# A two-tile feed-forward opened tile by tile with the tokens stationary, and the last norm's weight splits held back

## The reference

```python
def conv_glu_ffn(h, w_up_act, w_up_lin, w_conv, b_conv, w_down):   # first block, layers 0 and 1
    a = causal_depthwise_conv(h @ w_up_act, w_conv, b_conv)        # 3 taps over the tokens
    return (jax.nn.gelu(a) * (h @ w_up_lin)) @ w_down
...
def _swiglu(h, wg, wu, wd):                                        # second block
    return (jax.nn.silu(h @ wg) * (h @ wu)) @ wd
```

## Time and profile before

| | us |
|---|---|
| median of 3 runs | 2521.29 (2520.06 to 2528.47) |
| the profiled execution, its own time | 2527.51 |
| its span in the profile | 2525.7 |
| TensorE busy in it | 2431.3 |
| DVE busy in it | 1676.3 |
| ACT busy in it | 1080.5 |

### The profile page before, as it was taken

One profiled execution on the slowest core, in us unless ns is written; L12 is line 12 of the kernel. 1 busy time (PEld: TensorE's weight loads), 2 busy tenths in 40 slices (PEclk: granted clock), 3 DMA queues, 4 the chain that ended last, 5 costly groups with the idle time before them and its releaser, 6 DMA issues.

```text
span 2525.7 us, 34847 instructions
## 1 busy us (share of the span) xinstructions
PE 2431.3 (96%) x13166; PEld 2048.0 (81%) x13166; DVE 1676.3 (66%) x2618; ACT 1080.5 (43%) x1850; POOL 393.7 (16%) x431
## 2 busy tenths in 40 slices
PE   6899999999999999999979999999999999999998
PEld 5678987779989888887648888888888888787997
DVE  6957886857995776777865464566465566356454
ACT  4556545566554213237745322224322224345543
POOL 1111101111111201115851110110100110001101
PEclk9999999999999999999989999999999999999999
DMA  8755886646783654453212363442353444432662
GB/s 313 249 171 189 291 305 213 211 145 228 255 279 117 204 188 167 173 178 93 67 34 84 133 185 133 152 175 99 128 197 125 160 170 113 123 91 74 197 196 92
DMA packets 135880, 422.57 MB, mean 167 GB/s; under 512 B 28448, under 2 KB 32672, under 8 KB 135712
## 3 DMA queue, kind: packets, MB, share of 16 engines
q1 hardware_dynamic: 135152, 418.55, 49.0%
q10 hardware_dynamic: 560, 1.79, 0.2%
HBM read 419.17 MB, written 1.11 MB: 166 GB/s over the span
## 4 chain that ended last, share of the span: by engine, by line
PE 66%; DVE 2%; ACT 1%; POOL 1%; issue 0%; POOLq 0%; DVEq 0%; ACTq 0%
PE ps L1141 20%; PE ps L1142 20%; PE ps L1143 20%; PE ps L1336 2%; PE ps L1324 1%; POOL ap L2208 1%; PE ps L1241 1%; PE ps L1293 1%; PE ps L1304 1%; DVE ps L2033 0%; PE ps L1359 0%; PE ps L1348 0%; ACT F L1458 0%; DVE sl L1687 0%; DVE hL L1776 0%
## 5 line engine op out<-in xcount | busy, mean ns | idle before, releaser
L1399 ACT ACTIVATE sh<-raw 128x1024 fp32r<-128x1024 f32 x534 | 551.5, 1043 | 916.9 <-PE ps L1143 884.4
L1141 PE MATMUL ps<-hH,sh 128*128 128x256 f32 (+1 forms) x2560 | 843.1, 329 | 3.9 <-DVE hL L1776 2.9
L1143 PE MATMUL ps<-hH,sl 128*128 128x256 f32 (+1 forms) x2560 | 838.4, 327 | 0.0
L1142 PE MATMUL ps<-hL,sh 128*128 128x256 f32 (+1 forms) x2560 | 838.3, 327 | 0.0
L1687 DVE TENSOR_TENSOR sl<-raw,sh 128x1024 fp32r<-128x1024 f32 x534 | 639.4, 1217 | 100.6 <-ACT sh L1399 100.0
L1141 PEld LDWEIGHTS ps<-hH,sh 128*128 128x128 f32 x2560 | 481.4, 188 | 55.7 <-issue 8.1
L1143 PEld LDWEIGHTS ps<-hH,sl 128*128 128x128 f32 x2560 | 483.4, 189 | 48.1
L1142 PEld LDWEIGHTS ps<-hL,sh 128*128 128x128 f32 x2560 | 482.2, 188 | 49.1 <-issue 1.7
L1701 DVE CUSTOM_DVE_ANT_0 mjunk<-raw,cB,V 128x1024 bf16<-128x1024 f32 x384 | 499.0, 1299 | 27.0 <-DMA C<-in_cst 8.4
L2181 POOL TENSOR_TENSOR uLl<-F,uHh 128x256 fp32r<-128x256 f32 (+1 forms) x132 | 167.7, 1270 | 1185.0 <-ACT uHh L1576 1077.2
L1141 PE MATMUL ps<-sh,uHh 128*128 128x512 f32 x792 | 312.8, 395 | 2.1 <-DVE sl L1687 2.0
(11 more groups left out here) (164 smaller groups left out, 2047.3 us busy)
## 6 DMA issues: line engine op xcount, KB each, us to landing
raw<-in_w SPq DMA_DIRECT2D x752, 512.0 KB, 4.6
G<-gates SPq DMA_DIRECT2D x14, 512.0 KB, 6.3
raw<-in_w SPq DMA_DIRECT2D x16, 256.0 KB, 4.3
cB<-in_rpb SPq DMA_DIRECT2D x64, 64.0 KB, 2.6
raw<-in_w SPq DMA_DIRECT2D x4, 492.0 KB, 6.1
S<-in_rows SPq DMA_DIRECT2D x6, 256.0 KB, 3.3
X<-in_x ACTq DMA_DIRECT2D x1, 1024.0 KB, 11.9
X<-in_ctx SPq DMA_DIRECT2D x1, 1024.0 KB, 6.0
```

Source lines behind the costliest of these rows:

```text
L1141: self.e.matmul(out, lh, rh, start=start, stop=False)
L1142: self.e.matmul(out, lh, rl, start=False, stop=False)
L1143: return self.e.matmul(out, ll, rh, start=False, stop=stop)
L1399: self.e.activation(self.m["sh"][k % SPL][:, 0:w], self.m["raw"][r % RAW][:, 0:w], ACT.Copy).then_inc(self.sems["w_hi"], 1)
```

## The change

1. `by_tile` opens the two-tile feed-forwards in place of 14 fillers, `finish_norms()` and 5 fillers. It takes the first four 128-feature chunks of both weight matrices as 8 units of two row blocks x 512 columns, and multiplies with h stationary, tile by tile, as `down` does: units 0 to 3 (first matrix) and 4, 5 (second) for tile 0, then all for tile 1 in between with the rest of tile 0. Tile 1's turn and hsplit (`finish_norms`) stand behind the third part. Each [128 tokens, 512 features] result is copied from its bank to an S buffer (`utok`: tile 0 on ACT, tile 1 on DVE) and turned by four transposes into the banks that the products used to fill (`uturn`), two chunks to a bank.
2. In `ffn1` chunks 4 to 21 follow as products as before. The convolution and gelu of chunks 0 to 3 are put into chunks 4 and 5; the last transposes stand behind chunk 4's first product. In `ffn2` chunks 0 to 3 have their silu and multiplication ahead of chunk 4's products.
3. The fillers ahead are 7 in `ffn1` and 14 in `ffn2`.
4. At the end of the mixers of the first block, uppers are held from tile 1's first w_out part to `by_tile`. One is let through behind tile 0's hsplit, which now stands ahead of tile 1's `gate2`, and one ahead of tile 1's scale, where the first one's lower stands too.

```diff
@@ norm_tile
+        if held:
+            self.add("lowers")
+            self.add("ready", n=1)
         ys = [self.place("S", j) if wide else self.next("PT", 2) for j in range(2)]
         self.add("scale", t=t, st=st, ys=ys, xs=[self.xs(t, 0), self.xs(t, 1)])
@@ gate_half
         self.first_parts()
         self.rms_close(st2[t], 2)
+        self.second_parts()
+        if held and t:
+            self.add("ready", n=1)
@@ mixer
                     part(kp, half, taken[(kp, half)], [i], i == 1, banks[half][i] if kp == 3 else None)
-                self.gate_half(i, half, banks[half][i], gid, AB, hid, st2)
+                    if i and not half and kp == 2:
+                        self.add("hold", on=True)
+                self.gate_half(i, half, banks[half][i], gid, AB, hid, st2, True)
@@ new
+    def by_tile(self, names, hid, warm):
+        take = lambda n, j: self.unit(True, [n + (k, 0, 512) for k in (2 * j, 2 * j + 1)])
+        def part(n, j, t, b, last):
+            self.add("down", unit=n, ks=[2 * j, 2 * j + 1], tiles=[(t, (t, b))], last=last, full=b if j == 3 else None,
+                     act=("h", hid), nk=KD)
+            if t:
+                self.pace()
...
+        self.warm(warm)
+        self.add("hold", on=False)
+        one, two = ([take(n, j) for j in range(4)] for n in names)
+        A, B = [self.bank(), self.bank()], [self.bank(), self.bank()]
+        for j in range(3):
+            part(one[j], j, 0, A[0], False)
+        self.finish_norms()
+        part(one[3], 3, 0, A[0], False)
+        for j in range(2):
+            part(two[j], j, 0, B[0], False)
+        SA0 = stage(0, A[0], "a")
+        to = [self.bank(), self.bank()]
+        for j in range(4):
+            part(one[j], j, 1, A[1], True)
+            if j == 1:
+                turned(0, SA0, to)
+        for j in range(2):
+            part(two[j], j, 1, B[1], True)
+        SA1 = stage(1, A[1], "v")
+        for j in range(2, 4):
+            part(two[j], j, 0, B[0], False)
+        turned(1, SA1, to)
+        SB0 = stage(0, B[0], "a")
+        for j in range(2, 4):
+            part(two[j], j, 1, B[1], True)
+        up = [self.bank(), self.bank()]
+        turned(0, SB0, up)
+        SB1 = stage(1, B[1], "v")
+        return to, up, lambda: turned(1, SB1, up)
@@ ffn1
-        self.warm(14)
-        self.finish_norms()
-        self.warm(5)
+        to, up, rest = self.by_tile((("w_up_act", l), ("w_up_lin", l)), hid, 7)
         self.aside += [lambda: None] * 8
...
-        for c in range(KF):
+        for c in range(4, KF):
             ba = self.product("w_up_act", l, c * 128, slice(0, 256), ("h", hid))
-            if late:
+            if c == 4:
+                rest()
+            if c in (4, 5):
+                while late:
+                    late.pop(0)()
+                begin(2 * c - 8, to[c - 4], up[c - 4], 0)
+            late.pop(0)()
+            bu = self.product("w_up_lin", l, c * 128, slice(0, 256), ("h", hid))
+            late.pop(0)()
+            if c in (4, 5):
+                begin(2 * c - 7, to[c - 4], up[c - 4], 256)
                 late.pop(0)()
...
+            begin(c, ba, bu, 0)
             self.pace(2)
@@ ffn2
-            self.warm(14)
-            self.finish_norms()
-            self.warm(5)
+            to, up, rest = self.by_tile((("ffn_w_gate_2", (l, half_i)), ("ffn_w_up_2", (l, half_i))), hid, 14)
...
+                if len(tiles) == 2 and cc < 4:
+                    ba, bu, o = to[c // 2], up[c // 2], 256 * (c % 2)
+                    if c == 0:
+                        rest()
...
@@ finish
+                    if split and held and not (real and n <= s["unit"]):
+                        if not more:
+                            break
+                        more -= 1
@@ Tensor
+    def uturn(self, s):
...
+        self.wait_ge(self.got("tok", s["S"]))
+        for c in range(4):
+            o = 256 * (c % 2) + 128 * t
+            x = self.e.transpose(self.buf(s["to"][c // 2])[:, o:o + 128], S[:, c * 128:(c + 1) * 128],
+                                 self.m["C"][:, C_ID:C_ID + 128])
@@ Scalar
+    def utok(self, s):
...
+        self.e.copy(self.buf(s["S"])[:, :], self.buf(s["b"])[:, :]).then_inc(self.sems["a_ps"], 1)
@@ Vector
+    def utok(self, s):
...
+        self.e.tensor_copy(self.buf(s["S"])[:, :], self.buf(s["b"])[:, :]).then_inc(self.sems["v_ps"], 1)
```

More of the change, by code:

```diff
@@ L207, in xs, with norm_tile @@
         return ("x", t, h, self.x_at[(t, h)])
-    def norm_tile(self, hid, t, AB, s, st=None, wide=False, lag=0, early=False):
+    def norm_tile(self, hid, t, AB, s, st=None, wide=False, lag=0, early=False, held=False):
         if st is None:
@@ L310, in products, with gate_half @@
         return [b for _, b in got]
-    def gate_half(self, t, half, b, gid, AB, hid, st2):
+    def gate_half(self, t, half, b, gid, AB, hid, st2, held=False):
         if half == 0:
@@ L331, in gate_half @@
                 st = self.rms_open(self.xs(t, 0), D)
-        self.norm_tile(hid, t, AB, 0, st, early=True)
+        self.norm_tile(hid, t, AB, 0, st, early=True, held=held and t)
     def bias_rows(self, row, gid, tiles, hid):
@@ L627, in ffn2 @@
                 begun = bool(head)
+                if len(tiles) == 2 and cc < 4:
+                    ba, bu, o = to[c // 2], up[c // 2], 256 * (c % 2)
+                    if c == 0:
+                        rest()
+                    g = dict(N=N, c=c, ba=ba, bu=bu, o=o, s=self.place("S", c % 2), f=self.next("F", 3), fid=fid, u=self.u_at)
+                    if late:
+                        late.pop(0)()
+                    self.add("glu2_a", **g)
+                    if c % 2:
+                        self.left(ba, bu)
+                    late.append(lambda g=g: self.add("glu2_b", **g))
+                    continue
                 if head:
@@ L900, in finish @@
         out, n, ctx, top, used, order, lower, loads = [], 0, False, 0, set(), [], [], []
+        held, more = False, 0
         for s in self.steps:
             real = "unit" in s and s["kind"] != "place"
+            if s["kind"] == "hold":
+                held, more = s["on"], 0
+                continue
+            if s["kind"] == "ready":
+                more += s["n"]
+            if s["kind"] == "lowers":
+                out += lower
+                lower = []
+                continue
             if real:
@@ L905, in finish @@
                 lower = []
-            if "unit" in s or "upto" in s:
+            if "unit" in s or "upto" in s or s["kind"] == "ready":
+                if s["kind"] == "ready":
+                    s["upto"] = len(self.units)
                 top = max(top, s["upto"] if "upto" in s else s["unit"] + 1)
@@ L1169, in warm @@
         self.done("mm", ("left", s["b"]))
+    def uturn(self, s):
+        t, S = s["t"], self.buf(s["S"])
+        if t == 0:
+            for b in s["to"]:
+                self.wait_ge(self.gone(b))
+        self.wait_ge(self.got("tok", s["S"]))
[3 more added lines that the diff above has]
+                                 self.m["C"][:, C_ID:C_ID + 128])
+        x.then_inc(self.sems["tr"], 1)
+        self.done("tr", ("left", s["S"]), *([("full", b) for b in s["to"]] if t else []))
     def proj(self, s):
@@ L1978, in oscale @@
         self.done("v_sb", ("os", s["mid"], s["kd"], s["i"]))
+    def utok(self, s):
+        if s["on"] != "v":
+            return
+        self.wait_ge(self.got("full", s["b"]))
+        self.wait_ge(self.gone(s["S"]))
+        self.e.tensor_copy(self.buf(s["S"])[:, :], self.buf(s["b"])[:, :]).then_inc(self.sems["v_ps"], 1)
+        self.done("v_ps", ("left", s["b"]), ("tok", s["S"]))
     def glu1_a(self, s):
         l, c, fid = s["l"], s["c"], s["fid"]
-        S, pa = self.buf(s["s"]), self.buf(s["ba"])
+        S, pa = self.buf(s["s"]), self.buf(s["ba"])[:, s["o"]:s["o"] + 256]
         self.wait_ge(self.got("glu_a", fid, c))
```

47 lines of the change are left out of this document (30 added, 17 removed).

## The result

The changed kernel takes 2542.47 us (median of 6 runs, 2540.23 to 2543.43) against 2522.44 (median of 6, 2520.06 to 2528.47): a ratio of 1.0079, with an interval of 1.0065 to 1.0093. It is 20 us slower; the forecast was 2513.5, with 2506 to 2518.5 as its range and 0.05 for "slower".

The account below looks back on a forecast made before the run. TensorE, 96% busy, was taken to set the time behind layer 0's opening, DVE behind layer 1's. Gains 6.2 - 0.8 + 2.4 = 7.8 us, taken from the median 2521.3, gave 2513.5; range 2506 to 2518.5.

Parts of the forecast that it names:

- slower: Rival: the openings' matmuls run at the lower clock, 1.2 GHz, 22 us a place, up to 2579; chance 0.05.
- What A owes later: Layer 0's feed-forward: DVE's deferred convolution and gelu of chunks 0 to 3 are repaid at 0.87 us a chunk, costing nothing.
- A's margin: Layer 0's feed-forward: DVE ends unit 16's lower 1.5 us before TensorE wants it (8.6 before the change).
- the queue at B: DVE's work behind layer 1's opening: 8.0 us of idle counted, unit 16's lower at 620.1, TensorE stalling some 4.6 us.
- DVE without gaps of its own: Sign in layer 1's feed-forward: DVE runs gapless while TensorE idles 4 to 5 us for a lower.
- Place A: End of layer 0's mixer, before its two-tile feed-forward: gains 6.2 us, bounds 4.8 to 7.2.
- Place B: The same place in layer 1: loses 0.8 us as DVE decides; bounds +6.9 and -3.5.
- Place C: Before the last feed-forward, its norm unchanged: gains 2.4 us (1.4 to 2.9).
- A is eaten too: Rival: DVE's debt passes the 1.5 us margin in layer 0, TensorE stalls at unit 16, about 2518; chance 0.17.
- The Trainium skill's drain: Layer 1's silu table load: 1.38 us of drain per switch would lengthen the ping-pong by 1.4, losing 2.2 there.
- the gates' transfer: Layer 1: SP waits 8.8 us for the gates' columns ahead of weight loads, starving ACT 7.29; now four chunks later.

Follow-up runs that it names:

- e1: Changed kernel with the limit put back: the steps letting an upper through no longer raise the modulation columns' limit; 2513.47 us, ratio 0.997 to the kernel before.
- e6: Kernel before with the new opening and its norm in layer 1 alone, the limit put back; 2521.70 us, ratio 1.0002.
- e3: Kernel before with the opening by tile in the last feed-forward only; 2517.69 us, ratio 0.9989.
- e2: Kernel before plus the raised limit alone, so columns place the next upper from layer 0's first product on; 2538.01 us, ratio 1.0065.
- e4: Changed kernel with SP's fetch of the first block's feed-forward gates put three chunks behind its send; 2537.39 us, ratio 1.0063.

## Why the prediction was wrong

**The step that failed** is in "What A owes later": "DVE's saturated period is (624.02 - 620.51) = 3.5 us for a chunk without a modulation column, and 6.04 with one of two streams". These periods belong to an order of lowers, multiplication and convolution that the change does not keep. I took `ready` for "one upper let through", as the change says, and not also for a raised limit that stays. With the periods went "DVE wins back 5.65 - 3.5 - 1.28 = 0.87 us a chunk" (measured: it loses 0.1), and with them both A's margin and the queue at B. None of my rivals had it: the "slower" one was the clock in the openings, and it stayed at 1.00 there. Of the prediction's signs it is "DVE without gaps of its own" that the changed kernel fails, with 0.94 us in each chunk.

**What held, once the order was right (e1).** The total: 2513.5 forecast, 2513.47 measured. That is in part luck, since the terms differ as follows.

- *Place A* was to gain 6.2, with the opening's end 30.3 us behind tile 0's transposes. e1 has 31.1 (last transposes at 235.99, 0.35 for them, one product of 2.8 inside). Tile 1 is ready 15.6 us behind those transposes, not 14.9, and TensorE, through with tile 0's parts 0.7 later than forecast, waits 0.94 for it, as forecast. Against the profiled execution of before the gain is 5.4; at equal pitch it is 3.9 to 4.6, because the eight products replaced cost 21.8 rather than 22.6.
- *Place B*: a wait of 4.6 us for unit 16's lower, 26.9 us behind the opening's end, was forecast. e1 has 4.57, at 610.80, 26.7 behind 584.1. The forecast for the whole place was 0.8 lost; e1 and e6 have between 0.3 lost and 3.9 won, so better. A loss that I had not priced is the clock behind that wait: 0.66 in the 5 us from 610.
- *Place C*: 2.4 forecast, 2.4 in the changed kernel and in e3, at the slower pitch for the kernel before.
- *The rival "A is eaten too"* has the right place (unit 16's wait is at 255.23 in the changed kernel, with 0.63 us) and the wrong size: not a debt once, but a rate below TensorE's for the rest of the stage.
- *The Trainium skill's drain* beside ACT_TABLE_LOAD (ScalarE: Activation LUTs, What ACT_TABLE_LOAD costs) would, by an estimate, have put e1's wait at 6.0 instead of 4.57; the trace agrees with the row and not with that figure. In e1 too the silu's table load starts 0.02 us behind ACT's previous end, and the silu 0.01 behind the load.

**Why 20 us and not 10.** This is argued from the waits, and only its part on the transfer was run by itself. The order costs little where DVE has a lead (e2, layer 0). The openings by tile spend that lead, so each later delay falls on TensorE at once: the gates' transfer (e4: 5 us), and behind the longest waits 2 to 3 us each of lower clock (at 319.82, 628.42 and 698.50).

## What to carry to other kernels

A period read from a trace is the period of one order of instructions: before it is used for the kernel after, write out one chunk of each engine's queue in the new plan, since here 0.94 us of idle in each chunk came from one lower that moved by one place. A planner's helper step that changes a running maximum works on everything behind it; look where its effect ends. And a lead of a helper engine is a store: a change that spends it should be priced with everything that the lead used to cover.

## What the runs showed of the hardware

TensorE has two pitches at the full clock, 0.1133 and 0.1178 us for 256 columns, 0.2289 and 0.2334 for 512. TensorE keeps one of them for some us up to hundreds, and changes at waits (in the kernel before at the one that ends at 661.15), but also without one (there at 1076, between matmuls of one kind). It is not set by the kernel: the kernel before and e3 have the same steps in the first block, and from 600 to 630 one starts 267 matmuls and the other 257. First the kernel before, then e3:

```profile
600.00:630.00 30.00, 30.00 (x267) 30.00 (x266) 24.75 (x37) 20.53 (x29) 4.74 (x6) 1.00 0.80 285
```

```profile
600.00:630.00 30.00, 30.00 (x257) 30.00 (x256) 23.98 (x36) 21.49 (x29) 4.92 (x5) 1.00 0.82 296
```

On a feed-forward of 36 products and 264 wider matmuls that is 5 us, about the scatter of the runs; two stretches of different executions can be compared only at equal pitch. What chooses it stays open. The second surprise is the price of a wait in clock, and that it varies. Behind the 4.03 us at 319.82 TensorE had 0.50 in the next 5 us. Behind the wait near the end of layer 1 it had 0.66 in the kernel before (2.02 us, at 757.31), in e6 (2.01) and in e4 (3.04), and 1.00 in e1 (2.00) and in the changed kernel (3.05 us). Before, and then the changed kernel:

```profile
757.31:762.31 5.00, 5.00 (x15) 4.03 (x16) 3.40 (x5) 0.69 (x2) 0.75 (x2) 0.66 0.81 291
```

```profile
777.50:782.50 5.00, 5.00 (x22) 4.12 (x23) 4.39 (x6) 1.49 (x5) 0.83 (x3) 1.00 0.75 245
```

When a wait costs this and when not, stays open.
